# The 36 lead rows of V at the end of the V loop instead of evenly among the direct rows

## The chip, the core and the metric

The kernel runs on one core of a Trainium2 chip. The metric is the device time of one execution in microseconds (us). The changed kernel is timed in the same way as the kernel before.

## The reference

One encoder layer over two sequences (256 and 512 tokens, width 1024, treated as 6 tiles of 128 tokens): a norm, a projection to neighbourhood attention and retention heads, an output projection, a residual; then a second norm and a PEER layer (product-key expert retrieval), which is where this change lies:

```python
def block(args):
    xt, e, g = args              # tokens, 128 chosen experts of 16384 each, their gates
    ue = u[e]
    a = jax.nn.gelu(jnp.einsum('td,tkd->tk', xt, ue))
    ve = v[e]
    return jnp.einsum('tk,tkd->td', g * a, ve)
```

The experts stand in 128 rows of 128 experts each (`u` and `v` have 16384 x 1024 elements, float32).

## The kernel before, in words

The 768 tokens are two halves of 384 (3 tiles). PEER is computed in two ways.

**Scores of U.** In 256 steps TensorE multiplies one row of U (128 experts) with one half of the tokens: steps 0 to 127 for half 0, steps 128 to 255 for half 1. A step is 8 blocks of K by 3 products, since each operand is split into a high and a low part (`sp_hi`, `u_lo`; `ht_hi`, `ht_lo`): 24 matmuls of 384 columns (`scores`). ScalarE splits off the high part (`u_hi`), GpSimd the low part for steps up to 129 and VectorE from then on (`u_part`), and ScalarE applies the gelu into `act_g`, which has two buffers.

**Half 0 is sparse.** Its activations go to DRAM (`acts`), and each token's 128 chosen ones are gathered back. A *visit* n (384 of them: 3 tiles of tokens by 128 choices) is: GpSimd gathers the chosen V row of each of 128 tokens (`pick_v` into one of six `picked` slots, after visit n - 6 is done), and one activation per token (`pick_act` into `a_got`, 16 visits ahead); VectorE multiplies the row by its weight and adds it to `acc` or `acc_odd` (L1398).

**Half 1 is dense.** TensorE multiplies, for each of the 128 rows of V, the weights of all 384 tokens (activation times gate, `w_f`) with the row (`add_experts`): 3 tiles by 2 halves of the columns by 3 products, 18 matmuls of 512 columns. Its sums stay in PSUM through the whole loop.

**Lead rows and direct rows.** Steps 128 to 163 (rows 0 to 35 of half 1, `LEAD = 36`) are scored before the V loop, and their activations are stored to DRAM (`lead_acts`); these are the lead rows. In the V loop over q = 0 to 127 the row is `rows[q]`. For a lead row TensorE only runs `add_experts(q)`, and SyncE loads its activations back (`act_in`). For a direct row (36 to 127) TensorE first runs the score step of the next direct row and then `add_experts(q)`; the weights come straight from `act_g`.

**What sets the order.** All engines are programmed by hand and each runs its own instructions in order; semaphores join them. In a pass q of the V loop

- VectorE: a visit, `w_f` (L1416), a visit if the row has three, `w_lo` (L1421), for a direct row `u_lo` (L1433) of the row after next, a visit if the row has two or more, then `v_lo` (L1427) of q + 1.
- ScalarE: `w_hi` of q and then `v_hi` of q + 1, each of which waits until TensorE has ended the V matmuls that last read the same buffer (`y_done`, two rows back); for a direct row also the gelu of the next row and a `u_hi`.
- TensorE: for a direct row the scores of the next direct row, then `add_experts(q)`, which waits for `v_lo` and `w_lo` of q.
- SyncE (the SP queue): loads V for q + 2 after `v_lo` of q, the gates for q + 2 after `w_f` of q (`g_in`), the activations of the lead row two further on, and for a direct row a U row.
- GpSimd: only the gathers of the visits, with no tie to q but the `picked` slots.

`row_visits` says how many visits a row has: 3 for each direct row, and for a lead row 1, 2 or 3 (rows 0 and 3 three, rows 1, 2, 4, 5, 6 and those divisible by three from 9 on two, the others one). They sum to the 330 visits that are left when the loop begins (54 are made during the lead steps).

After the loop come the last sums, roots and outputs of half 0, then those of half 1.

Of the kernel before, what the change touches and what calls it, by code (L numbers as in the profile page):

```python
# [26 lines left out]
PEER_HEADS, TOPK, N_KEYS = 8, 16, 128  # L27
# [13 lines left out]
LEAD = 36  # L41
# [30 lines left out]
def encoder_program(nc, a):  # L72
# [3 lines left out]
    with ctx:  # L76
# [147 lines left out]

        rows, placed = [], {}
        for q in range(N_KEYS):
            early = q * LEAD % N_KEYS < LEAD
            n = sum(1 for row in rows if (row < LEAD) == early)
            rows.append(n if early else LEAD + n)
            placed[rows[q]] = q  # L230
# [1344 lines left out]
```

## Time and profile before

| | us |
|---|---|
| median of 3 runs | 2622.14 (2612.92 to 2632.96) |
| the profiled execution | 2621.9 |
| its span (first to last instruction) | 2620.1 |
| TensorE busy, matmuls (PE) | 2394.0 |
| VectorE busy (DVE) | 1719.4 |
| GpSimd busy (POOL) | 1356.0 |
| ScalarE busy (ACT) | 871.7 |

The profile is of one execution. Times in its rows are in us from the start of the span; a duration with "mean" is in ns. PE stands for TensorE's matmuls, PEld for its weight loads, DVE for VectorE, ACT for ScalarE, POOL for GpSimd, SP and SPq for SyncE and its DMA queue. Matmuls overlap one another in the trace (each row shows its latency), so what a group of matmuls costs is read from the starts. A row's bracket at the end is the engine's idle time before the instruction, and what ended it; "issue" is a gap in which the engine waited for nothing that the profile shows. L714 is line 714 of the kernel, the helper in which all score and V matmuls are issued. The V loop runs from about 1604 to 2603 us.

### The profile page before, as it was taken

How to read it: one execution, taken by the hardware profiler on the slowest of the kernel's cores; microseconds unless marked ns; L12 is line 12 of the kernel's file. 1: busy time of each engine (PE TensorE's matmuls, PEld its weight loads, DVE VectorE, ACT ScalarE, POOL GpSimd, SP SyncE). 2: the span in 40 equal slices, each digit the busy share in tenths (PEclk: the TensorE clock that was granted, in tenths of full speed). 3: DMA queues.
4: the chain of work that ended last, by engine and by line, in shares of the span. 5: the costliest groups of instructions: out<-in, count | busy, mean ns of one | idle time of the engine just before them, and what ended most of it. 6: DMA issues, size and time to landing. Idle time of an engine off the chain costs nothing.

```text
span 2620.1 us, 33731 instructions
## 1 busy us (share of the span) xinstructions
PE 2394.0 (91%) x12633; PEld 2158.4 (82%) x12633; DVE 1719.4 (66%) x3313; ACT 871.7 (33%) x1356; POOL 1356.0 (52%) x954
## 2 busy tenths in 40 slices
PE   5999998899999999999986877999999899999997
PEld 5977776799999999998976776887888788888886
DVE  4145437331798888555094956877887778777877
ACT  4234322232333333343332322333333333333333
POOL 1001130000266656644585545788778877888773
PEclk9999999989999999999998998999999999999998
DMA  4111102112455555537749598998999999988996
GB/s 143 65 47 46 56 33 81 57 65 89 151 171 171 176 185 180 166 130 219 231 151 356 176 303 286 322 356 312 323 321 325 316 320 325 322 317 302 330 320 232
DMA packets 233602, 555.10 MB, mean 212 GB/s; under 512 B 32064, under 2 KB 123200, under 8 KB 231776
## 3 DMA queue, kind: packets, MB, share of 16 engines
q1 hardware_dynamic: 164592, 345.04, 38.7%
q0 software_dynamic: 68848, 207.91, 22.7%
q8 instruction: 101, 1.65, 0.3%
q14 instruction: 61, 0.50, 0.1%
HBM read 483.90 MB, written 68.94 MB: 211 GB/s over the span
## 4 chain that ended last, share of the span: by engine, by line
PE 43%; POOL 26%; DVE 11%; DMA 8%; issue 8%; ACT 3%; SPq 1%; DVEq 0%; ACTq 0%; POOLq 0%
PE ps L714 25%; POOL a_got L466 12%; POOL picked L461 12%; PE ps L757 10%; DMA raw<-in_experts 4%; DVE hot_a L1341 4%; DMA picked<-in_experts,vidx 3%; POOL u_lo L472 2%; DVE hot_b L1337 2%; PE ps L793 2%; DVE acc_odd L1398 1%; PE ps L814 1%; ACT sp_hi L634 1%; DVE u_lo L1433 1%; PE ps L803 1%
## 5 line engine op out<-in xcount | busy, mean ns | idle before, releaser
L714 PE MATMUL ps<-ht_hi,sp_hi 128*128 128x384 f32 x2048 | 710.3, 347 | 48.6 <-DVE u_lo L1433 25.1
L714 PE MATMUL ps<-ht_hi,u_lo 128*128 128x384 f32 x2048 | 693.1, 338 | 0.0
L714 PE MATMUL ps<-ht_lo,sp_hi 128*128 128x384 f32 x2048 | 692.2, 338 | 0.0
L461 POOL DMA_INDIRECT picked<-in_experts,vidx x384 | 475.8, 1239 | 207.8 <-issue 108.1
L472 POOL TENSOR_TENSOR u_lo<-raw,sp_hi 128x1024 fp32r<-128x1024 f32 x130 | 340.6, 2622 | 418.6 <-ACT sp_hi L634 418.6
L466 POOL DMA_INDIRECT a_got<-acts,aidx x384 | 483.7, 1260 | 117.1 <-issue 117.0
L714 PEld LDWEIGHTS ps<-ht_hi,sp_hi 128*128 128x128 f32 x2048 | 389.3, 190 | 75.1 <-POOL u_lo L472 40.3
L714 PEld LDWEIGHTS ps<-ht_lo,sp_hi 128*128 128x128 f32 x2048 | 389.6, 190 | 3.6
L714 PEld LDWEIGHTS ps<-ht_hi,u_lo 128*128 128x128 f32 x2048 | 388.7, 190 | 0.0
L714 PE MATMUL ps<-v_hi,w_hi 128*128 128x512 f32 x768 | 311.3, 405 | 73.7 <-DVE w_lo L1421 57.8
L643 ACT ACTIVATE act_g<-ps 128x384 f32<-128x384 f32 x256 | 125.6, 491 | 609.4 <-PE ps L714 604.4
L714 PE MATMUL ps<-v_lo,w_hi 128*128 128x512 f32 x768 | 309.1, 402 | 0.0
L714 PE MATMUL ps<-v_hi,w_lo 128*128 128x512 f32 x768 | 309.1, 402 | 0.0
L634 ACT ACTIVATE sp_hi<-raw 128x1024 fp32r<-128x1024 f32 x256 | 269.5, 1053 | 103.7 <-DMA raw<-in_experts 103.6
L1398 DVE SCALAR_TENSOR_TENSOR acc<-picked,wts,acc 128x1024 f32<-128x1024 f32 x192 | 246.3, 1283 | 84.6 <-DMA picked<-in_experts,vidx 83.9
L1398 DVE SCALAR_TENSOR_TENSOR acc_odd<-picked,wts,acc_odd 128x1024 f32<-128x1024 f32 x189 | 243.1, 1286 | 67.2 <-DMA picked<-in_experts,vidx 66.7
L714 PEld LDWEIGHTS ps<-v_hi,w_hi 128*128 128x128 f32 x768 | 149.7, 195 | 116.2 <-issue 87.3
L1433 DVE TENSOR_TENSOR u_lo<-raw,sp_hi 128x1024 fp32r<-128x1024 f32 x126 | 153.5, 1218 | 81.5 <-ACT sp_hi L634 81.5
L986 DVE TENSOR_TENSOR sp_lo<-raw,sp_hi 128x1024 fp32r<-128x1024 f32 x52 | 63.3, 1223 | 199.2 <-ACT sp_hi L500 190.9
L1427 DVE TENSOR_TENSOR v_lo<-v_raw,v_hi 128x1024 fp32r<-128x1024 f32 x128 | 156.3, 1221 | 38.1 <-ACT v_hi L651 38.0
L757 PE MATMUL ps<-ht_hi,sp_hi 128*128 128x384 f32 x512 | 175.9, 344 | 5.3 <-DVE sp_lo L986 2.9
L688 ACT ACTIVATE w_hi<-w_f 128x384 fp32r<-128x384 f32 x128 | 67.1, 524 | 328.7 <-DVE w_f L1416 325.6
(183 smaller groups left out, 3431.4 us busy)
## 6 DMA issues: line engine op xcount, KB each, us to landing
raw<-in_experts SPq DMA_DIRECT2D x256, 512.0 KB, 3.9
v_raw<-in_experts SPq DMA_DIRECT2D x128, 512.0 KB, 5.5
raw<-in_front SPq DMA_DIRECT2D x52, 512.0 KB, 3.2
acts<-act_g SPq DMA_DIRECT2D x128, 192.0 KB, 3.5
gates<-stage SPq DMA_DIRECT2D x24, 1024.0 KB, 9.5
g_in<-gates SPq DMA_DIRECT2D x128, 192.0 KB, 5.4
lead_acts<-act_g SPq DMA_DIRECT2D x36, 192.0 KB, 5.4
act_in<-lead_acts SPq DMA_DIRECT2D x36, 192.0 KB, 5.6
```

The costliest lines, as they stand in the source:

```text
L461: pool.indirect_dma_start(picked[n % SLOTS][:, :], None, v_rows, bass.IndirectOffsetOnAxis(ap=vidx[:, n // P, n % P:n % P + 1], axis=0)).t ...
L466: pool.indirect_dma_start(a_got[:, n // P, n % P:n % P + 1], None, acts, bass.IndirectOffsetOnAxis(ap=aidx[:, n // P, n % P:n % P + 1], ax ...
L472: pool.tensor_tensor(u_lo[:, step % 2], raw[:, step % 2], sp_hi[:, step % 2].bitcast(F32), ALU.subtract).then_inc(S["u_lo"], 1)
L634: act.activation(sp_hi[:, step % 2], raw[:, step % 2], ACT.Copy).then_inc(S["u_hi"], 1)
L643: act.activation(act_g[:, step % 2], ps[:, step % 2, 0:HALF], ACT.Gelu_apprx_tanh).then_inc(S["gelu_done"], 1)
L688: act.activation(w_hi[:, q % 2], w_f[:, q % 2], ACT.Copy).then_inc(S["w_hi_ready"], 1)
L714: last = pe.matmul(out, l, r, start=start and k == 0, stop=stop and k == 2, skip_group_check=True)
L757: last = pe.matmul(ps[:, n % 2, 0:HALF], w, x, start=e == 0, stop=e == 23, skip_group_check=True)
L1341: last = dve.tensor_scalar(hot_a[:, g % HOT, q, :], s["iota"][:, :], idx_t[:, 0, t % 2, tok:tok + 1], idx_t[:, 2, t % 2, tok:tok + 1], ALU ...
L1398: last = dve.scalar_tensor_tensor(o[:, :], row, w, o[:, :], ALU.mult, ALU.add)
L1427: dve.tensor_tensor(v_lo[:, q % 2], v_raw[:, q % 2], v_hi[:, q % 2].bitcast(F32), ALU.subtract).then_inc(S["v_lo"], 1)
L1433: dve.tensor_tensor(u_lo[:, step % 2], raw[:, step % 2], sp_hi[:, step % 2].bitcast(F32), ALU.subtract).then_inc(S["u_lo_dve"], 1)
```

## The change

One line of the table that places the rows:

```diff
         rows, placed = [], {}
         for q in range(N_KEYS):
-            early = q * LEAD % N_KEYS < LEAD
+            early = q >= N_KEYS - LEAD
             n = sum(1 for row in rows if (row < LEAD) == early)
             rows.append(n if early else LEAD + n)
             placed[rows[q]] = q
```

Before, the order is 0, 36, 37, 38, 1, 39, 40, 41, 2, 42, 43, 3, and so on, to 35, 126, 127: a lead row after every two or three direct ones. Now it is 36 to 127, then 0 to 35. The number of visits of each row stays, and so do all instructions; GpSimd's order is the same, and those of TensorE, VectorE, ScalarE and SyncE are changed in the V loop.

VectorE at the beginning of the V loop, before (`acc_146` is the accumulator of the first tile of tokens, `picked_139` to `picked_144` are the six slots): the first pass is lead row 0 with three visits, the second is direct row 36.

```order
 L1427 TENSOR_TENSOR v_lo<-v_raw,v_hi 128x1024
 L1374 TENSOR_TENSOR wts<-a_got,sgate 128x8
 L1398 SCALAR_TENSOR_TENSOR acc_146<-picked_139,wts,acc_146 128x1024
 L1416 TENSOR_TENSOR w_f<-act_in,g_in 128x384
 L1398 SCALAR_TENSOR_TENSOR acc_odd<-picked_140,wts,acc_odd 128x1024
 L1421 TENSOR_TENSOR w_lo<-w_f,w_hi 128x384
 L1398 SCALAR_TENSOR_TENSOR acc_146<-picked_141,wts,acc_146 128x1024
 L1427 TENSOR_TENSOR v_lo<-v_raw,v_hi 128x1024
 L1398 SCALAR_TENSOR_TENSOR acc_odd<-picked_142,wts,acc_odd 128x1024
 L1416 TENSOR_TENSOR w_f<-act_g,g_in 128x384
```

The same place now:

```order
 L1427 TENSOR_TENSOR v_lo<-v_raw,v_hi 128x1024
 L1374 TENSOR_TENSOR wts<-a_got,sgate 128x8
 L1398 SCALAR_TENSOR_TENSOR acc_146<-picked_139,wts,acc_146 128x1024
 L1416 TENSOR_TENSOR w_f<-act_g,g_in 128x384
 L1398 SCALAR_TENSOR_TENSOR acc_odd<-picked_140,wts,acc_odd 128x1024
 L1421 TENSOR_TENSOR w_lo<-w_f,w_hi 128x384
 L1433 TENSOR_TENSOR u_lo<-raw,sp_hi 128x1024
 L1398 SCALAR_TENSOR_TENSOR acc_146<-picked_141,wts,acc_146 128x1024
 L1427 TENSOR_TENSOR v_lo<-v_raw,v_hi 128x1024
 L1398 SCALAR_TENSOR_TENSOR acc_odd<-picked_142,wts,acc_odd 128x1024
```

The first pass is a direct one: its weights come from `act_g`, and a `u_lo` stands between `w_lo` and the third visit.

VectorE at the end of the V loop, before (`acc_148` is the accumulator of the third tile; L1402 joins the two accumulators after the last visit): direct row 127 with three visits.

```order
 L1427 TENSOR_TENSOR v_lo<-v_raw,v_hi 128x1024
 L1398 SCALAR_TENSOR_TENSOR acc_odd<-picked_142,wts,acc_odd 128x1024
 L1416 TENSOR_TENSOR w_f<-act_g,g_in 128x384
 L1398 SCALAR_TENSOR_TENSOR acc_148<-picked_143,wts,acc_148 128x1024
 L1421 TENSOR_TENSOR w_lo<-w_f,w_hi 128x384
 L1398 SCALAR_TENSOR_TENSOR acc_odd<-picked_144,wts,acc_odd 128x1024
 L1402 TENSOR_TENSOR acc_148<-acc_148,acc_odd 128x1024
```

The same place now, lead rows 33, 34 and 35:

```order
 L1421 TENSOR_TENSOR w_lo<-w_f,w_hi 128x384
 L1398 SCALAR_TENSOR_TENSOR acc_odd<-picked_142,wts,acc_odd 128x1024
 L1427 TENSOR_TENSOR v_lo<-v_raw,v_hi 128x1024
 L1398 SCALAR_TENSOR_TENSOR acc_148<-picked_143,wts,acc_148 128x1024
 L1416 TENSOR_TENSOR w_f<-act_in,g_in 128x384
 L1421 TENSOR_TENSOR w_lo<-w_f,w_hi 128x384
 L1427 TENSOR_TENSOR v_lo<-v_raw,v_hi 128x1024
 L1398 SCALAR_TENSOR_TENSOR acc_odd<-picked_144,wts,acc_odd 128x1024
 L1402 TENSOR_TENSOR acc_148<-acc_148,acc_odd 128x1024
 L1416 TENSOR_TENSOR w_f<-act_in,g_in 128x384
 L1421 TENSOR_TENSOR w_lo<-w_f,w_hi 128x384
```

A lead row has a visit between `v_lo` and `w_f`, and a second one, where it has it, between `w_lo` and the next `v_lo`. The last visit and the joining of the accumulators now stand ahead of the last row's weights.

## Rows read from the trace of the kernel before

**Rows 1.** The page: busy time of each engine and its share of the span.

```profile
PE 2394.0 (91%) x12633; PEld 2158.4 (82%) x12633; DVE 1719.4 (66%) x3313; ACT 871.7 (33%) x1356; POOL 1356.0 (52%) x954
```

**Rows 2.** The page: the chain that ended last, shares of the span by line.

```profile
PE ps L714 25%; POOL a_got L466 12%; POOL picked L461 12%; PE ps L757 10%; DMA raw<-in_experts 4%; DVE hot_a L1341 4%; DMA picked<-in_experts,vidx 3%; POOL u_lo L472 2%; DVE hot_b L1337 2%; PE ps L793 2%; DVE acc_odd L1398 1%; PE ps L814 1%; ACT sp_hi L634 1%; DVE u_lo L1433 1%; PE ps L803 1%
```

**Rows 3.** Waits of GpSimd, 1700 to 2560 us: total, times, longest.

```profile
POOL a_got L466 <- issue: 85.5, 280, 0.3
POOL picked L461 <- issue: 82.4, 270, 0.3
```

**Rows 4.** Waits of all engines, 1605 to 2600 us.

```profile
PE ps L714 <- DVE w_lo L1421: 57.8, 35, 4.3
```

**Rows 5.** Timeline of VectorE at three places: start, duration, instruction.

```profile
1604.23 1.28 DVE L1398 SCALAR_TENSOR_TENSOR acc<-picked,wts,acc 128x1024 f32<-128x1024 f32 x1
...
2492.54 1.28 DVE L1398 SCALAR_TENSOR_TENSOR acc_odd<-picked,wts,acc_odd 128x1024 f32<-128x1024 f32 x1 [0.91 <-DMA picked<-in_experts,vidx]
...
2598.05 0.55 DVE L1421 TENSOR_TENSOR w_lo<-w_f,w_hi 128x384 fp32r<-128x384 f32 x1
```

**Rows 6.** VectorE, groups from 2492.5 to 2600 us: busy, mean ns, idle.

```profile
L1398 DVE SCALAR_TENSOR_TENSOR acc_odd<-picked,wts,acc_odd 128x1024 f32<-128x1024 f32 x19 | 24.4, 1285 | 8.0 <-DMA picked<-in_experts,vidx 7.8
L1398 DVE SCALAR_TENSOR_TENSOR acc<-picked,wts,acc 128x1024 f32<-128x1024 f32 x18 | 23.2, 1287 | 4.9 <-DMA picked<-in_experts,vidx 4.9
```

**Rows 7.** Timeline of TensorE's matmuls, starts of three groups.

```profile
2002.67 0.47 PE L714 MATMUL ps<-v_hi,w_hi 128*128 128x512 f32 x1 [1.02 <-DVE w_lo L1421]
...
2006.87 0.33 PE L714 MATMUL ps<-ht_hi,sp_hi 128*128 128x384 f32 x1
...
2011.05 0.39 PE L714 MATMUL ps<-v_hi,w_hi 128*128 128x512 f32 x1
```

**Rows 8.** Timeline of VectorE from 2000.8 to 2016 us.

```profile
2000.82 0.55 DVE L1416 TENSOR_TENSOR w_f<-act_in,g_in 128x384 f32<-128x384 f32 x1
2001.96 0.56 DVE L1421 TENSOR_TENSOR w_lo<-w_f,w_hi 128x384 fp32r<-128x384 f32 x1 [0.59 <-ACT w_hi L688]
2002.91 1.23 DVE L1427 TENSOR_TENSOR v_lo<-v_raw,v_hi 128x1024 fp32r<-128x1024 f32 x1 [0.39 <-ACT v_hi L651]
2004.05 1.28 DVE L1398 SCALAR_TENSOR_TENSOR acc<-picked,wts,acc 128x1024 f32<-128x1024 f32 x1
2005.25 0.60 DVE L1416 TENSOR_TENSOR w_f<-act_g,g_in 128x384 f32<-128x384 f32 x1
...
2007.44 1.22 DVE L1433 TENSOR_TENSOR u_lo<-raw,sp_hi 128x1024 fp32r<-128x1024 f32 x1
...
2011.53 1.29 DVE L1398 SCALAR_TENSOR_TENSOR acc_odd<-picked,wts,acc_odd 128x1024 f32<-128x1024 f32 x1 [0.42 <-DMA picked<-in_experts,vidx]
...
2015.81 1.29 DVE L1398 SCALAR_TENSOR_TENSOR acc<-picked,wts,acc 128x1024 f32<-128x1024 f32 x1 [2.53 <-DMA picked<-in_experts,vidx]
```

**Rows 9.** DMA, 1700 to 2560 us: queues (packets, MB, share), V loads.

```profile
q0 software_dynamic: 49249, 146.85, 48.3%
q1 hardware_dynamic: 47711, 129.13, 42.8%
...
v_raw<-in_experts SPq DMA_DIRECT2D x110, 512.0 KB, 5.5
```

**Rows 10.** Timeline of GpSimd from 2011 to 2015 us.

```profile
2011.09 0.94 POOL L461 DMA_INDIRECT picked<-in_experts,vidx  x1 [0.30 <-issue]
...
2013.94 0.94 POOL L461 DMA_INDIRECT picked<-in_experts,vidx  x1 [0.31 <-issue]
```

**Rows 11.** Timeline of ScalarE from 2001 to 2008 us.

```profile
2001.84 1.04 ACT L651 ACTIVATE v_hi<-v_raw 128x1024 fp32r<-128x1024 f32 x1
...
2007.13 1.06 ACT L651 ACTIVATE v_hi<-v_raw 128x1024 fp32r<-128x1024 f32 x1 [0.72 <-PE ps L714]
```

**Rows 12.** Busy time by stretch; the last three: granted clock, DMA share, GB/s.

```profile
1700.00:2560.00 860.00, 806.39 (x3870) 710.23 (x3869) 673.83 (x723) 281.07 (x377) 689.04 (x561) 0.98 0.91 322
```

**Rows 13.** Timeline of VectorE after the loop.

```profile
2607.59 3.48 DVE L1495 TENSOR_TENSOR x2d<-ps,x2d 128x1024 f32<-128x1024 f32 x3
```

## The prediction

> **What bounds the kernel now.** I read the busy line of the page first [rows 1]: TensorE is busy in 91% of the span and looks like the bound. The chain that ended last contradicts this for the last part of the kernel: a quarter of it is GpSimd's two gathers, `picked` and `a_got` [rows 2]. So the question is which engine sets the pace of the V loop, the stretch from 1604 us on, in which the order of the 128 V rows matters.
>
> GpSimd's waits between 1700 and 2560 us [rows 3] are only the gap of 0.3 us that stands before every gather: 168 us over 550 gathers. Nothing else is long enough to be named. GpSimd never stops, while TensorE waits 57.8 us for `w_lo` in the loop [rows 4]. One visit (a gathered V row for each of 128 tokens, and a gathered activation) costs GpSimd two gathers, and 384 visits are to be made.
>
> The pace: the first visit of the loop (number 54 of 0 to 383) starts at 1604.23 us [rows 5]. Number 347 starts at 2492.54 us, since 19 + 18 = 37 multiply-adds start from there on [rows 5, 6]. That is 293 visits in 888.3 us, 3.03 us each.
>
> TensorE's own price: the 18 V matmuls of a row take 4.2 us (2002.67 to 2006.87), the 24 score matmuls 4.2 us (2006.87 to 2011.05) [rows 7]. A direct row needs both, 8.4 us, a lead row 4.2 us. All rows need 92 x 8.4 + 36 x 4.2 = 924 us; from the first visit of the loop to the last `w_lo` (2598.05 us [rows 5]) it is 994. GpSimd asks 3 x 3.03 = 9.1 us for the three visits of a direct row, more than TensorE's 8.4. In the kernel before, one lead row comes for 2.56 direct ones: 3.56 rows hold 9.2 visits, 27.8 us of GpSimd, against 25.7 us of TensorE. TensorE runs ahead, waits about 1.6 us at each lead row (57.8 us in 35 waits), and GpSimd sets the time.
>
> **The change, part by part.** It moves rows, and adds or removes nothing. Loads, splits, matmuls and visits stay; GpSimd's order of instructions is the same. Each row keeps its visits: 3 for a direct row; for leads 3, 2, 2, 3, 2, 2, 2 (rows 0 to 6, 17 visits), then 1, with 2 for a row divisible by 3 (rows 7 to 35: 29 rows, 37 visits, 1.28 each).
>
> *Direct rows, 92 in a run.* GpSimd asks 9.1 us, TensorE 8.4, VectorE 3 x 1.28 + 2 x 1.22 + 2 x 0.55 = 7.4 [rows 8]. DMA stands below them: the software queue takes 48.3% of 860 us for 280 visits, 1.48 us each, the hardware queue 42.8% for 129 MB, 2.85 us per MB [rows 9]; a direct row with three visits and 1.25 MB of U, V and gates asks 8.0 us. So GpSimd stays the bound, and TensorE waits 0.7 us in each row. The leads, which gave GpSimd nothing to do beyond its pace but TensorE less work, no longer stand among them: TensorE loses 0.7 us 92 times, and keeps 36 short rows for the end.
>
> *Does GpSimd's pace itself move?* A gather takes 0.94 us while VectorE rests (2013.94 us [rows 10]; VectorE is idle for 2.53 us until 2015.81 [rows 8]), so a visit is at least 2 x (0.94 + 0.30) = 2.48 us; 0.55 of the 3.03 us come from gathers stretched beside VectorE's work. Per visit, that work is one multiply-add of 1.28 us and 1.24 us of splits and weights ((128 x 2.32 + 90 x 1.22) / 330). In the first 293 visits after the change the latter is (92 x 3.54 + 7 x 2.32) / 293 = 1.17 us. If splits and weights alone stretch gathers, 0.07 x 0.55 / 1.24 x 293 = 9 us are saved; if multiply-adds stretch them as much, half of it. The gather at 2011.09 us took 0.94 us beside the multiply-add of 2011.53 [rows 8, 10], which speaks for the first. Bounds 0 and 9, taken 8: visit 347 starts at 2492.5 - 8 = 2484.5 us.
>
> [...]
>
> *Lead rows 0 to 6* hold 2.4 visits each and stay at GpSimd's pace. Visit 347 is now the first of lead row 7 (54 + 92 x 3 + 17 = 347), so rows 0 to 6 lie within the count.
>
> *Lead rows 7 to 35, the new stage.* A row asks GpSimd for 1.28 x 3.03 = 3.9 us, DMA for 1.28 x 1.48 + 0.92 MB x 2.85 = 4.5, TensorE for 4.2. But no score matmuls stand between the V groups now, so what ScalarE and VectorE do between them is no longer covered. The pieces [rows 8, 11]: `w_f` to `w_lo` 1.14 us (2000.82, 2001.96), `v_hi` to `v_lo` 1.07 (2001.84, 2002.91), `v_lo` to the visit 1.14 (2004.05), visit to the next `w_f` 1.20 (2005.25). `v_hi` and `w_hi` are double, and those of row q+2 wait until TensorE has ended row q. This closes a loop over two rows: TensorE starts (2002.67), ScalarE's waiting `v_hi` starts 4.46 us later (2007.13), then 1.07 + 1.14 + 1.20 + 1.14, then 0.71 from `w_lo` to TensorE (2001.96 to 2002.67). Sum 9.72 us, 4.86 per row. Eight rows have a second visit between `w_lo` and the next `v_lo`, where VectorE is free for 0.9 us of the 1.2 (counted from TensorE's start of the row, `w_lo` has ended at -0.71 + 0.5 = -0.2, and `v_lo` can start at 4.46 - 4.86 + 1.07 = 0.67), so each adds 0.3 us: mean (21 x 4.86 + 8 x 5.16) / 29 = 4.94 us. V loads land in a median of 5.5 us [rows 9] and the loop leaves them 9.7 - 1.1 - 1.2 = 7.4; but some are slower, and the granted clock is 0.98 and not 1 [rows 12]. I allow 0.16 us: 5.1 us per row. Bounds: 4.43, the serial part on ScalarE and VectorE alone (`w_f` 2000.82 to 2005.25), and 5.6, if half of the V loads land 3 us late.
>
> *The queue.* On SP each lead row issues loads of V, gates and `act_in`, no U; the first two `act_in` loads come before the loop as now and lie ready for 92 rows. None is put behind a wait it did not have.
>
> *The tail.* Before: from the last `w_lo` (2598.05 [rows 5]) to the end 22.0 us, in which the last visit, the sum of the two accumulators and three outputs stand ahead of the additions at 2607.59 [rows 13], 9.5 us behind `w_lo`. Now the last visit stands ahead of the last weights, and the additions can start some 5.7 us behind `w_lo` (2 us of sums and roots, 3.7 of outputs): 22.0 - 3.8 = 18.2 us.
>
> **Sum.** 2484.5 + 2.3 (visit 347 to `w_lo` of row 7: 1.20 + 1.14) + 28 x 5.1 + 18.2 = 2647.8 us of span, and 1.8 us around it (the profiled execution took 2621.9 us with a span of 2620.1): **2650 us**. That execution stands at the median of the three runs (2622.1), so nothing is corrected. It is 28 us, 1.1%, slower.
>
> **The rivals.**
> 1. *No loss that can be measured.* If the loop over two rows does not bind, leads run at 4.43 us: 2484.5 + 2.3 + 124 + 18.2 + 1.8 = 2631 us. Or DMA and not GpSimd is the bound: its share is 0.91 [rows 12], the bytes do not change, and the end stays near 2620. Against the first stands the `v_hi` that waits for TensorE [rows 11]; against the second, that a gather with VectorE idle takes its shortest time under full DMA load.
> 2. *The lead stage stretches.* With a gap of 0.7 us in each row TensorE could be granted 1.2 instead of 2.4 GHz. The V matmuls of a row then take 4.2 us more, 2.1 us per row in the loop; over half of the stage 14 x 2.1 = 29 us, 2679 us. With late V loads, at 5.6 us per row, it is 2664. Against it: the granted clock is 0.98 with waits of 1.6 us at each lead row now.
> 3. *Faster: direct rows free GpSimd.* If a gather fell to 1.1 us there (2.8 us per visit), TensorE's 8.4 us would be the pace, visit 347 would start at 1604.2 + 293 x 2.8 = 2425 and the end be 2590. That needs 68 us saved where I find 8; it decides at 2.91 us per visit (visit 347 some 28 us earlier than I put it), below which the change is no loss. Nothing speaks for it: VectorE is busy for 7.4 of 9.1 us in a direct row, as densely as now (674 of 860 us).
>
> **How the numbers follow.** Forecast (2639 to 2662) 0.57; no loss (2620 to 2639) 0.21; stretch (2662 to 2688) 0.17; faster 0.05. About 1% (26 us) is what a measurement of this kernel can tell from no change. The line of 1% slower, 2648, lies within the forecast; 0.34 of its 0.57 go above it. Slower 0.34 + 0.17 = 0.51, same 0.23 + 0.21 = 0.44, faster 0.05. The range 2626 to 2684 leaves out the fast case, the DMA case and the far end of the stretch.
>
> **What would show it.** Right: GpSimd without waits until about 2480 us; TensorE waiting for `w_lo` 0.7 us in nearly each direct row; the 92nd row's visits done near 2433 us (17 visits before 2484.5); then GpSimd waiting for visits, leads 4.9 to 5.2 us apart, and `v_hi` waiting for TensorE. Wrong: leads 4.4 or over 5.6 us apart, `v_hi` waiting for its load, a clock well below 0.9 in the last 140 us, or direct rows 8.4 us apart.

## The result

The changed kernel is slower. Its median is 2673.1 us (2670.5 to 2691.1, 4 runs) against 2619.9 us (2612.9 to 2633.0, 4 runs) for the kernel before; the ratio is 1.022, with a 95% interval of 1.016 to 1.027. Timed again on another occasion (x4 below) it is 2669.9 against 2625.8 us, ratio 1.018 (1.014 to 1.023). I had forecast 2650 us, 1.1% slower, in a range of 2626 to 2684. So the time is in the range, but the loss of 53 us (44 in x4) is well above the 28 us forecast, and 2673 us stands where I had put the stretch of the lead stage (2662 to 2688, chance 0.17). A fifth execution of the changed kernel, of 2682.2 us, counts in the ratio and not in the median. The ratios, here and below, leave out executions more than 1.5% above the fastest of the same kernel, which are two of five in x1 and one of four in x8.

The profile taken with the result is of the execution of 2691.1 us, the slowest of the four. The one of x4 is of 2662.0 us. Both are used, and kept apart.

The page of the changed kernel, busy time of each engine and the chain by line, as [rows 1, 2]:

```profile
PE 2411.7 (90%) x12633; PEld 2160.4 (80%) x12633; DVE 1719.2 (64%) x3313; ACT 869.9 (32%) x1356; POOL 1380.3 (51%) x954
...
PE ps L714 22%; POOL a_got L466 12%; POOL picked L461 12%; PE ps L757 10%; DMA raw<-in_experts 5%; DVE hot_a L1341 4%; POOL u_lo L472 3%; DMA picked<-in_experts,vidx 2%; DVE hot_b L1337 2%; PE ps L793 2%; ACT sp_hi L634 1%; PE ps L814 1%; DVE acc L1398 1%; DVE acc_odd L1398 1%; DVE u_lo L1433 1%
```

The gathers' share of the chain is the same 12 + 12%. The matmuls' went from 25 to 22% of a longer span: nothing was added to TensorE's work, and what came is waiting.

GpSimd's waits from 1700 to 2560 us, as [rows 3], first profile of the changed kernel:

```profile
POOL a_got L466 <- issue: 83.0, 272, 0.3
POOL picked L461 <- issue: 80.3, 263, 0.3
POOL picked L461 <- DVE acc_odd L1398: 3.1, 8, 0.6
POOL picked L461 <- DVE acc L1398: 0.9, 2, 0.6
```

GpSimd has no waits but 4 us in the whole stretch, as forecast for the direct run. Then the same view of all engines in the lead stage, from x4 (2500 to 2640 us):

```profile
PE ps L714 <- DVE w_lo L1421: 18.4, 23, 1.5
POOL picked L461 <- DVE acc L1398: 16.8, 8, 4.2
...
POOL picked L461 <- DVE acc_odd L1398: 15.6, 13, 3.5
...
ACT v_hi L651 <- PE ps L714: 5.4, 8, 0.7
```

Here GpSimd waits 32 us for visits, and TensorE 18 us for `w_lo` in 23 rows: neither bounds the lead stage. (The first profile has 21 us for `w_lo` in 21 rows there, 2525 to 2668 us.) Three places of x4's VectorE timeline, as [rows 5]: the first visit of the loop, `w_lo` of lead row 7 (the 100th row), and `w_lo` of the last row.

```profile
1603.63 1.28 DVE L1398 SCALAR_TENSOR_TENSOR acc<-picked,wts,acc 128x1024 f32<-128x1024 f32 x1
...
2498.38 0.56 DVE L1421 TENSOR_TENSOR w_lo<-w_f,w_hi 128x384 fp32r<-128x384 f32 x1 [0.59 <-ACT w_hi L688]
...
2638.86 0.56 DVE L1421 TENSOR_TENSOR w_lo<-w_f,w_hi 128x384 fp32r<-128x384 f32 x1 [0.59 <-ACT w_hi L688]
```

Where the time went, in four profiles. The visits are numbered as in the prediction; visit 330 is the first after the direct run of the changed kernel. Each start is read from VectorE's timeline.

| | before | before again (x12) | after again (x4) | after |
|---|---|---|---|---|
| visit 54 starts | 1604.2 | 1603.3 | 1603.6 | 1606.0 |
| visit 330 starts | 2441.7 | 2434.4 | 2448.0 | 2472.0 |
| us per visit between | 3.03 | 3.01 | 3.06 | 3.14 |
| end of the span | 2620.1 | 2616.4 | 2660.2 | 2689.2 |
| from visit 330 to the end | 178.4 | 182.0 | 212.2 | 217.2 |
| lead rows 7 to 35, us per row | - | - | 5.02 | 5.14 |

Between x12 and x4, 30 us of the 44 come behind visit 330, where the changed kernel has its 36 lead rows with 54 visits, and the kernel before had the end of one direct row and 21 rows, 15 of them direct, with as many visits. The other 14 us are GpSimd's pace in the direct run. In the profile that came with the result the pace costs 30 us, and the lead stage 39.

### The profile page after: what moved, and what is told of

Its sections match the earlier page's. It is cut to its first block, busy times and chain, and to the rows that moved or that the text cites. A ratio compares the mean times of both kernels' runs of the same rounds, so it can differ in the third digit from the quotient of the medians.

```text
span 2689.2 us, 33731 instructions
## 1 busy us (share of the span) xinstructions
PE 2411.7 (90%) x12633; PEld 2160.4 (80%) x12633; DVE 1719.2 (64%) x3313; ACT 869.9 (32%) x1356; POOL 1380.3 (51%) x954
## 4 chain that ended last, share of the span: by engine, by line
PE 39%; POOL 27%; DVE 12%; DMA 9%; issue 8%; ACT 4%; SPq 0%; DVEq 0%; ACTq 0%; POOLq 0%
PE ps L714 22%; POOL a_got L466 12%; POOL picked L461 12%; PE ps L757 10%; DMA raw<-in_experts 5%; DVE hot_a L1341 4%; POOL u_lo L472 3%; DMA picked<-in_experts,vidx 2%; DVE hot_b L1337 2%; PE ps L793 2%; ACT sp_hi L634 1%; PE ps L814 1%; DVE acc L1398 1%; DVE acc_odd L1398 1%; DVE u_lo L1433 1%
## 5 line engine op out<-in xcount | busy, mean ns | idle before, releaser
L461 POOL DMA_INDIRECT picked<-in_experts,vidx x384 | 493.4, 1285 | 244.6 <-issue 108.9
L466 POOL DMA_INDIRECT a_got<-acts,aidx x384 | 489.2, 1274 | 117.0 <-issue 116.9
L714 PE MATMUL ps<-v_hi,w_hi 128*128 128x512 f32 x768 | 320.4, 417 | 119.8 <-DVE w_lo L1421 107.0
L714 PEld LDWEIGHTS ps<-v_hi,w_lo 128*128 128x128 f32 x768 | 152.3, 198 | 34.3
```

The source lines that it names most:

```text
L461: pool.indirect_dma_start(picked[n % SLOTS][:, :], None, v_rows, bass.IndirectOffsetOnAxis(ap=vidx[:, n // P, n % P:n % P + 1], axis=0)).t ...
L466: pool.indirect_dma_start(a_got[:, n // P, n % P:n % P + 1], None, acts, bass.IndirectOffsetOnAxis(ap=aidx[:, n // P, n % P:n % P + 1], ax ...
L714: last = pe.matmul(out, l, r, start=start and k == 0, stop=stop and k == 2, skip_group_check=True)
```

## The experiments

Times are medians; each ratio is to the kernel before, timed on the same chip. The executions of one kernel lie 4 to 17 us apart in most experiments, 22 in x4 and 36 in x10; those of the kernel before 12 to 35 us, by chip. In two kernels they part more widely: x1 took 2586 to 2596 or 2628 to 2635 us, x8 2574, 2603 or 2622 us. Profiles of both kinds exist for x1 alone (x1 and x11).

### x1 and x11: the same rows, the visits dealt out otherwise

```diff
-        row_visits = [3 if row >= LEAD else 1 for row in rows]
+        row_visits = [2 if row < LEAD or row % 5 == 0 else 3 for row in rows]
```

> The changed kernel (lead rows last) with the 330 visits of the V loop dealt out otherwise: every lead row has two, direct rows three, but those whose number is divisible by 5 two (18 of 92). Direct rows then hold 2.8 visits, lead rows 2. Theory (the time is lost because GpSimd, the bound in the direct run, has too little to do in the last 29 lead rows): GpSimd asks 2.8 x 3.1 = 8.7 us in a direct row and 6.1 us in a lead row, is never idle, and the time is that of the kernel before, 2610 to 2630 us. Rival 1 (lead rows in a run are slow by themselves, whatever visits they hold): 2655 us or more. Rival 2 (the loss is only the slower gathers of a run of direct rows, 3.14 us per visit against 3.03): 2640 to 2650 us.

Measured: 2587.7, 2586.1 and 2595.6 us, and 2628.3 and 2634.9 us; ratio 0.986 (0.984 to 0.988). The lead rows still stand last, and the whole loss is gone. More than that, the kernel is quicker than before. Neither rival holds. The slower two of the five are near the time of the kernel before, as the theory has it; the median of all five is 2595.6 us. The theory explains the return, not the gain, so the kernel was run once more for a profile of the quicker kind:

> x1 once more, since its profile is of an execution of 2635 us, while its others took 2586 to 2596 and 2628. Theory (two paces of GpSimd: gathers stretched while the direct run is GpSimd's, short once TensorE's regular beat leads): in a fast execution a visit costs 2.95 us or less in the direct run (8.3 us per row for 2.8 visits), a_got gathers take 1.1 us or less in the mean against 1.24 in the slow profile, and the lead stage takes the same in both. Rival (the lead stage is what differs): direct run as in the slow profile, lead rows under 5 us.

Measured: 2600.9 and 2586.1 us, on another chip than x1. GpSimd's groups from 1700 to 2360 us, first in x1 (the execution of 2634.9 us), then in x11 (2600.9 us): count, busy, mean ns, idle before.

```profile
L461 POOL DMA_INDIRECT picked<-in_experts,vidx x211 | 268.6, 1273 | 64.4 <-issue 61.9 <-DVE acc_odd L1398 2.4
L466 POOL DMA_INDIRECT a_got<-acts,aidx x212 | 263.2, 1241 | 64.7 <-issue 64.7
```

```profile
L461 POOL DMA_INDIRECT picked<-in_experts,vidx x224 | 259.3, 1158 | 101.1 <-issue 53.0 <-DVE acc_odd L1398 32.4 <-DVE acc L1398 15.7
L466 POOL DMA_INDIRECT a_got<-acts,aidx x224 | 230.6, 1030 | 68.5 <-issue 68.5
```

The activation gathers take 1241 ns in the mean in one and 1030 in the other, of the same program. Rows 36 to 91 of the loop stand 8.78 us apart in x1 (`w_lo` 1916.8 to 2399.5, 55 rows) and 8.31 in x11 (1918.0 to 2374.9), which is TensorE's price of a direct row. In x11 GpSimd waits 48 us for visits, in x1 2.4. The lead stage differs little (5.82 and 5.67 us per row). So the direct run has two paces: either GpSimd leads, and its gathers are stretched; or TensorE leads, and they are short. What makes a gather long or short is shown under x5 and x6.

### x2: the lead rows first

```diff
-            early = q >= N_KEYS - LEAD
+            early = q < LEAD
```

> The 36 lead rows at the beginning of the V loop instead of at the end, 3 visits in direct rows and 1 to 3 in lead rows as before. Theory (what costs is the clustering: GpSimd waits while lead rows with few visits pass, and bounds the direct rows): GpSimd idle in lead rows 7 to 35, then 276 visits at 3.1 us; as slow as with the leads last, 2650 to 2672 us, up to 15 us less because GpSimd enters the direct run six visits ahead. Rival (what costs is that the leads stand at the end of the program, where their loads, the last visits and the outputs meet): near the kernel before, 2615 to 2630 us.

Measured: 2660.4 us, ratio 1.014 (1.011 to 1.016). As the theory says; the end of the program has little to do with it. The waits of GpSimd while lead rows 7 to 35 pass (1660 to 1802 us):

```profile
POOL picked L461 <- DVE acc L1398: 32.4, 8, 12.3
POOL picked L461 <- DVE acc_odd L1398: 11.2, 14, 3.3
```

43.6 us of waiting for VectorE, lost at the beginning (12.3 of them in one wait), for which the direct rows behind pay: they go at GpSimd's pace to the end (9.19 us per row, `w_lo` 1802.0 to 2638.2 over 91 rows).

### x3: the loop over two rows made shorter

```diff
+                late = rows[q] < LEAD and row_visits[q] == 1
-                visits(1)
+                if not late:
+                    visits(1)
                 weights(q)
...
-                visits(row_visits[q] > 1)
+                visits(row_visits[q] > 1 or late)
```

> The changed kernel, in which a lead row with one visit makes it behind w_lo instead of between v_lo and w_f, so that the loop over two rows (v_hi, v_lo, visit, w_f, w_hi, w_lo, TensorE's group) is 1.2 us shorter for 20 of the last 29 rows. Theory (this loop sets the pace of the lead stage, 4.99 us per row in the changed kernel): 4.4 to 4.6 us per row, 10 to 15 us less than the changed kernel, which is 2673, so 2658 to 2663 us. Rival 1 (DMA sets the pace of the lead stage): 4.8 to 5.0 us per row, no change, 2670 us or more. Rival 2 (the picked rows arrive too late for an early visit): the gain is larger than 15 us, since the wait moves off the path as well.

Measured: 2660.9 us, ratio 1.013 (1.010 to 1.016); x4, on the same chip, 1.018. Lead rows 7 to 35 stand 4.69 us apart ((2635.3 - 2504.0) / 28) instead of 5.02, 9.2 us less in all, and the median is 8.9 us lower. The intervals overlap, so the time alone would not settle it; the rows' distance does. 4.69 us is more than the 4.4 to 4.6 us expected: `v_hi` waits for its V load in five rows here (5.5 us), in one in x4 (0.9 us). That is 0.16 us per row, which would account for it; it is not shown that nothing else does. (The 4.99 us for the changed kernel in the expectation was misread: it is 5.14 in the first profile.)

### x4 and x12: both kernels again

x4 is the changed kernel without an edit, x12 the kernel before.

> The changed kernel once more, on the same chip as the others. The profile that came with the result is of an execution of 2691 us, 18 us above the median of 2673. Theory: a visit costs 3.05 to 3.10 us in the direct run of a usual execution (3.14 in that profile), lead rows 7 to 35 stand 4.9 to 5.0 us apart in every execution, and the time is 2668 to 2676 us. Rival: the direct run is as slow as in that profile, and the lead stage is what varies.

> The kernel before once more, for its pace in another execution. Theory: 3.00 to 3.06 us per visit from visit 54 to 330, a_got gathers 1.24 us in the mean, GpSimd without waits, 2612 to 2633 us, the spread of its time following from the pace (330 visits times 0.03 us are 10 us).

Measured: x4 2669.9 us (2657.9 to 2680.3), x12 2618.3 us, one execution. The direct run is what varies most between the two profiles of the changed kernel: 3.06 and 3.14 us per visit, which is 22 us over 276 visits. The lead stage varies less, 5.02 and 5.14 us per row, 3.5 us over 28 rows, a little above the 4.9 to 5.0 expected: in the first profile `v_hi` waits for its V load in six rows (5.0 us), in x4 in one (0.9 us). GpSimd's activation gathers from 1700 to 2360 us, in x12, x4 and the first profile of the changed kernel:

```profile
L466 POOL DMA_INDIRECT a_got<-acts,aidx x218 | 265.8, 1219 | 66.6 <-issue 66.6
```

```profile
L466 POOL DMA_INDIRECT a_got<-acts,aidx x214 | 260.9, 1219 | 65.3 <-issue 65.3
```

```profile
L466 POOL DMA_INDIRECT a_got<-acts,aidx x207 | 268.5, 1297 | 63.2 <-issue 63.2
```

They take 1219, 1219 and 1297 ns; the V gathers (not shown) 1198, 1263 and 1274 ns. The pace follows the gathers' lengths.

### x5 and x6: what stretches a gather

x5 computes the low part of U in the V loop for 64 of 1024 columns; x6 shortens the multiply-adds of the visits in the same way.

```diff
+                n = D_MODEL if step < FIRST_DIRECT + 2 else 64
-                dve.tensor_tensor(u_lo[:, step % 2], raw[:, step % 2], ...
+                dve.tensor_tensor(u_lo[:, step % 2, 0:n], raw[:, step % 2, 0:n], ...
```

> The changed kernel with the low part of U in the V loop computed for 64 of its 1024 columns (the rest of u_lo is left as it was, so the scores of the direct rows are not the reference's): VectorE has 1.1 us less of two-input subtraction in each direct row, everything else is as before. In the second profile of the changed kernel a visit costs 3.06 us in the direct run, of which 2.48 are two gathers of 0.94 and their gaps. Theory (splits and weights stretch the gathers, 0.44 us per us; multiply-adds do not): 0.16 us less, 2.90 us per visit, 45 us less over 276 visits. Rival 1 (all two-input work stretches alike, 0.22 us per us): 2.98 us per visit, 22 us less. Rival 2 (the pace is not GpSimd's gathers but the landing of their data): 3.06 as before.

```diff
-                    last = dve.scalar_tensor_tensor(o[:, :], row, w, o[:, :], ALU.mult, ALU.add)
+                    n_cols = 64 if n >= VISITS - left else D_MODEL
+                    last = dve.scalar_tensor_tensor(o[:, 0:n_cols], row[:, 0:n_cols], w, o[:, 0:n_cols],
+                                                    ALU.mult, ALU.add)
```

> The changed kernel with the multiply-adds of the visits in the V loop done for 64 of 1024 columns (so the outputs of half 0 are not the reference's): VectorE has 1.1 us less in each visit; gathers are whole. Theory (multiply-adds hardly stretch the gathers): a visit stays at 3.0 to 3.06 us in the direct run, and the only gain is in the lead stage, whose loop over two rows holds one visit: 4.3 instead of 5.0 us per row, 20 us less in all. Rival (the port rule: a multiply-add with two SBUF inputs blocks the descriptor writing like a split): 0.24 us less per visit, 2.82, so that TensorE's 8.4 us per row bounds, 65 us less in the direct run besides.

Measured: x5 2626.7 us, 43 us below x4 (another chip, on which the kernel before took the same 2625.8 us), and 2.90 us per visit in the direct run (1608.5 to 2408.8 us, 276 visits), which is the theory's number. x6 (two executions) 2556.6 us, 113 us below x4: 2.75 us per visit (1606.1 to 2365.2), TensorE's pace, and 4.54 us per lead row. GpSimd's activation gathers in x6, same stretch as above:

```profile
L466 POOL DMA_INDIRECT a_got<-acts,aidx x238 | 236.0, 992 | 72.9 <-issue 72.9
```

992 ns, near the 940 of a gather beside an idle VectorE. The expectation for x6 fell: multiply-adds do stretch gathers, as its rival said. A multiply-add became 1.00 us shorter (1.28 to 0.28 us), and a visit at least 0.31 us (TensorE's pace hides the rest); in x5 a split became 1.00 us shorter (1.22 to 0.22 us), which is 0.33 us per visit, and a visit 0.16 us. So both count.

How they count is in the traces. VectorE and then GpSimd in x4:

```profile
1991.80 1.28 DVE L1398 SCALAR_TENSOR_TENSOR acc<-picked,wts,acc 128x1024 f32<-128x1024 f32 x1 [1.68 <-DMA picked<-in_experts,vidx]
...
1996.81 1.28 DVE L1398 SCALAR_TENSOR_TENSOR acc<-picked,wts,acc 128x1024 f32<-128x1024 f32 x1 [0.88 <-DMA picked<-in_experts,vidx]
...
1998.47 1.22 DVE L1433 TENSOR_TENSOR u_lo<-raw,sp_hi 128x1024 fp32r<-128x1024 f32 x1
```

```profile
1991.17 0.94 POOL L461 DMA_INDIRECT picked<-in_experts,vidx  x1 [0.30 <-issue]
1992.41 1.48 POOL L466 DMA_INDIRECT a_got<-acts,aidx  x1 [0.30 <-issue]
...
1997.05 1.86 POOL L461 DMA_INDIRECT picked<-in_experts,vidx  x1 [0.30 <-issue]
1999.21 1.30 POOL L466 DMA_INDIRECT a_got<-acts,aidx  x1 [0.30 <-issue]
```

The gather at 1991.17 starts while VectorE is idle and takes 0.94 us, though a multiply-add starts 0.63 us behind it. The one at 1992.41 meets that multiply-add with 0.67 us left (it ends at 1993.08) and takes 1.48. The one at 1997.05 meets a multiply-add with 1.04 us left and takes 1.86; the one at 1999.21 a split with 0.48 us left, and takes 1.30. Each time it is what is left of VectorE's instruction plus 0.81 or 0.82 us. So a gather is stretched only by the instruction that is under way when it starts; one that starts later does not matter.

All fourteen profiles show this between 1700 and 2360 us, where they hold 6046 gathers. 2513 of them meet a VectorE instruction that began at least 0.1 us before them and has at least 0.13 us left: in 2498 the length is what is left plus 0.82 us, within 0.03, with multiply-adds and splits alike. 1535 meet none with as much left, and none that starts within 0.1 us of them: all take 0.93 to 0.97 us, but one of 1.21. The other 1998 start within 0.1 us of the start of a VectorE instruction, and some of these are short and some long. The stretch of the pace is thus a matter of when the gathers start, and the two rates above are means over such starts.

### x7 and x8: GpSimd relieved, in both orders

Activations are gathered further ahead: two per visit while the 54 visits before the V loop are made, 0.83 per visit in it.

```diff
+            got = CHUNK
             for n in range(VISITS):
-                for k in ((CHUNK + 2 * n, CHUNK + 2 * n + 1) if n < CHUNK else (n + 2 * CHUNK,)):
-                    if k < VISITS:
-                        pick_act(k)
+                upto = min(VISITS, CHUNK + 2 * (n + 1) if n < 54 else max(118 + (n - 54) * 83 // 100, n + 12))
+                for k in range(got, upto):
+                    pick_act(k)
+                got = max(got, upto)
```

(and 12 semaphores `a_in` instead of 4).

> The kernel before (lead rows spread), but GpSimd gathers the activations further ahead: two per visit while the 54 visits before the V loop are made, where it waits some 100 us for VectorE, and then 0.83 per visit, so that it enters the loop 64 visits ahead in activations instead of 16. In the loop a visit costs it one V gather and 0.83 activation gathers for the most part, about 2.75 us instead of 3.03. Theory (GpSimd bounds the V loop of the kernel before): 2.8 x 2.75 = 7.7 us per average direct row, so TensorE's 924 us become the bound of the loop: 2560 to 2590 us. Rival 1 (GpSimd is not the bound, DMA is): no change, 2615 to 2625. Rival 2 (the lead steps become longer, since the earlier gathers load the DMA queues there): what the loop gains is lost before it, 2600 or more.

> The same with the lead rows last. Theory: the direct run goes at TensorE's 8.4 to 8.5 us per row (92 rows, 778 us), then lead rows 0 to 6 at 6.5 and 7 to 35 at 5.0 us (bound by the loop over two rows, 0.8 us per row above TensorE's price): 1604 + 778 + 45 + 145 + 21 = 2593 span, 2585 to 2600 us, 10 to 25 us behind the spread order, where the changed kernel is 45 us behind it. So placing the leads last costs less once GpSimd has slack. Rival (the cost of the placement is independent of GpSimd's pace): again 45 us behind the spread order.

Measured: spread, 2585.4 us (2575.4 to 2588.8), ratio 0.984 (0.977 to 0.990); leads last, 2588.9 us (2573.6, 2574.8, 2603.1 and 2621.7), ratio 0.986 (0.975 to 0.996). The difference between the orders, 44 us without this, cannot be told from zero with it: GpSimd's slack is what decides what the placement costs. In both, visit 54 starts 2 to 6 us later than without the earlier gathers (1609.7 and 1607.6 us), so little is lost before the loop. The difference between the orders is less than the 10 to 25 us that I expected. In the two profiles the direct run with the leads last wastes none of TensorE's time, and the spread order does. The stretch from 1700 to 2360 us in x7, x8 and x4: busy time of PE, PEld, DVE, ACT, POOL, then granted clock, DMA share, GB/s.

```profile
1700.00:2360.00 660.00, 643.30 (x3148) 573.17 (x3147) 549.13 (x594) 228.88 (x308) 530.85 (x423) 0.99 0.96 345
```

```profile
1700.00:2360.00 660.00, 660.00 (x3340) 601.23 (x3339) 560.87 (x588) 230.53 (x316) 497.55 (x438) 1.00 0.96 343
```

```profile
1700.00:2360.00 660.00, 613.73 (x3001) 547.80 (x3001) 503.62 (x530) 210.67 (x286) 529.73 (x428) 0.98 0.90 311
```

In x8 TensorE is busy in all 660 us, with 3340 matmuls against 3001 in x4. That gathers are short there is seen in VectorE's and GpSimd's timelines of x8 around 2010 us:

```profile
2002.54 1.28 DVE L1401 SCALAR_TENSOR_TENSOR acc<-picked,wts,acc 128x1024 f32<-128x1024 f32 x1
2004.87 0.56 DVE L1419 TENSOR_TENSOR w_f<-act_g,g_in 128x384 f32<-128x384 f32 x1 [1.05 <-ACT act_g L646]
...
2010.77 1.28 DVE L1401 SCALAR_TENSOR_TENSOR acc_odd<-picked,wts,acc_odd 128x1024 f32<-128x1024 f32 x1
2013.18 0.62 DVE L1419 TENSOR_TENSOR w_f<-act_g,g_in 128x384 f32<-128x384 f32 x1 [1.13 <-ACT act_g L646]
2013.72 1.27 DVE L1401 SCALAR_TENSOR_TENSOR acc<-picked,wts,acc 128x1024 f32<-128x1024 f32 x1
```

```profile
2003.66 0.98 POOL L467 DMA_INDIRECT a_got<-acts,aidx  x1 [0.30 <-issue]
...
2011.96 0.94 POOL L467 DMA_INDIRECT a_got<-acts,aidx  x1 [0.30 <-issue]
2013.21 0.94 POOL L462 DMA_INDIRECT picked<-in_experts,vidx  x1 [0.30 <-issue]
```

VectorE waits 1.13 us for `act_g`, TensorE's product, in nearly every row (84 us in 76 rows from 1700 to 2360 us), and an activation gather starts as that gap opens: at 2011.96 us, where the multiply-add has 0.09 us left, and one row earlier at 2003.66, where it has 0.16, 8.30 us apart like the two `w_f`. In x8 159 of 198 activation gathers are shorter than 1 us, in x4 90 of 213; in x11 it is 167 of 224, in x1 78 of 211. When GpSimd leads, VectorE waits for picked rows instead, at places that change. That the regular beat is what puts the starts of gathers there is argued from these rows, and fits x1 and x11; no run forced the one pace or the other with all else equal.

### x9 and x10: both placed on top

x9 has x8's gathers and x1's visits, x10 x8's gathers and x3's late visit.

> Lead rows last, visits dealt out as in x1 (2.8 per direct row, 2 per lead row) and activations gathered ahead as in x8. In x8's profile the direct run goes at TensorE's 8.30 us per row with three visits each, and executions fall into two groups (2574 and 2603 to 2622 us). Theory (GpSimd bounds only while its gathers are stretched; with 2.8 visits instead of 3 per direct row it has 0.5 us more slack per row): all executions in the fast group; lead rows with two visits are bound by VectorE at 5.2 us, so 2570 to 2580 us. Rival (the two groups have nothing to do with GpSimd's slack): a spread of 30 us or more again, median 2585 to 2600.

> x8 with the late visit of x3 in lead rows with one visit. Theory (the two changes add, since one acts on the direct run and the other on the lead stage): 9 us less than x8 in the same group of executions, 4.7 instead of 5.0 us per lead row: 2563 to 2568 us where x8 has 2574. Rival (the lead stage is bound by loads once GpSimd is ahead): 5.0 us per lead row as in x8, 2573.

Measured: x9 2594.9 us (2593.5 to 2598.8), ratio 0.988 (0.984 to 0.993): the four executions agree within 5 us, as the theory says, but 15 us above its figure, at a median that its rival gave. The direct run is at 8.31 us per row (`w_lo` 1907.5 to 2364.4, 55 rows), the lead rows with two visits at 5.83 instead of the 5.2 I had from VectorE's work. VectorE's and TensorE's waits there, 2410 to 2570 us:

```profile
PE ps L717 <- DVE w_lo L1424: 35.7, 23, 7.3
...
DVE wts L1377 <- DMA a_got<-acts,aidx: 13.1, 4, 6.3
```

Thirteen us are waiting for activations that were not gathered far enough ahead any more (four waits of VectorE), and the DMA share is 0.95 from 2430 to 2560 us. x10: 2582.2 us (2563.7 to 2599.9), ratio 0.983 (0.976 to 0.991), and 4.76 us per lead row ((2555.6 - 2422.2) / 28) against 5.02 in x8, 7 us less. The mechanism is as expected, but the median does not stand clear of x7's and x8's. x10, x7 and x8 are all quicker than both kernels of this case; which of them is best these runs can't tell.

## Why the prediction was right, and where it was off

**The bound.** Right. GpSimd sets the pace of the direct run, not TensorE, though TensorE is busy in over 90% of it: x7 and x8 take GpSimd's work and nothing else out of the loop, and 40 us (x7) and 81 us (x8 against x4, on another chip) go.

**Where the loss comes from.** Right for 30 of the 44 us between x12 and x4, and shown from two sides. The visits of the direct rows are too many for GpSimd, those of the last lead rows too few to keep it busy. x1 moves visits, not rows, and the loss is gone; x2 moves the rows to the other end, and most of it stays. The other 14 us (30 in the first profile) are GpSimd's pace in the direct run, for which I had forecast a small gain.

**The lead stage.** The loop over two rows gave 4.94 us per row, with 0.16 allowed for late loads and the clock; measured 5.02 and 5.14. ScalarE's and VectorE's timelines of x4 show the distances that the sum was made of:

```profile
2603.32 0.56 DVE L1421 TENSOR_TENSOR w_lo<-w_f,w_hi 128x384 fp32r<-128x384 f32 x1 [0.59 <-ACT w_hi L688]
2604.33 1.23 DVE L1427 TENSOR_TENSOR v_lo<-v_raw,v_hi 128x1024 fp32r<-128x1024 f32 x1 [0.45 <-ACT v_hi L651]
2605.48 1.28 DVE L1398 SCALAR_TENSOR_TENSOR acc_odd<-picked,wts,acc_odd 128x1024 f32<-128x1024 f32 x1
2606.68 0.55 DVE L1416 TENSOR_TENSOR w_f<-act_in,g_in 128x384 f32<-128x384 f32 x1
2607.82 0.56 DVE L1421 TENSOR_TENSOR w_lo<-w_f,w_hi 128x384 fp32r<-128x384 f32 x1 [0.59 <-ACT w_hi L688]
```

```profile
2608.49 1.06 ACT L651 ACTIVATE v_hi<-v_raw 128x1024 fp32r<-128x1024 f32 x1 [0.70 <-PE ps L714]
```

From `w_lo` 2603.32 to the next, 2607.82, it is 4.50 us: the serial part on ScalarE and VectorE (4.43), and behind it the `v_hi` at 2608.49 that had to wait 0.70 us for TensorE, so that the next row takes 5.24 (to 2613.06). These two rows together make 9.74, the 9.72 of the sum. Behind a row with two visits the distance is 5.15 (2613.06 to 2618.21), and `v_hi` waits for nothing there: VectorE's own instructions are the path. The mean is within 0.1 us of the forecast in x4. x3, which takes the visit out of the loop, and x6, which shortens it, both move the distance. I had the number of second visits slightly wrong: the rows 0 to 6 hold 16 visits, not 17, and nine rows from 7 on have a second visit, not eight; visit 346 and not 347 is then the first of row 7, worth 3 us.

**GpSimd's pace.** The step that failed. I took 8 us off before visit 347, since there is less splitting per visit in direct rows. Measured, visit 347 starts at 2500.5 us in x4 and 2525.9 in the first profile, not at 2484.5: 16 and 41 us later. A visit costs 3.06 and 3.14 us in the direct run, where it cost 3.03 and 3.01. Two things were wrong. I took it that splits and weights alone stretch gathers, at 0.44 us per us. x6 and the rows of x4 above show that multiply-adds count alike. The gather of 0.94 us beside a multiply-add, on which I rested this ([rows 8, 10]), started at 2011.09 us, 0.44 us ahead of the multiply-add of 2011.53, and so says nothing about it. And the pace does not follow from the amount of work: what counts is what VectorE has under way when a gather starts. For starts at random moments I estimate, from the 0.82 us and VectorE's durations of 1.28, 1.22 and 0.55 us, a stretch of 0.38 us per gather in either order; measured are 0.29 and 0.27 in the two profiles of the kernel before (from the means), 0.30 in x4 and 0.35 in the first profile. So the amount of work would have moved nothing. The same program runs at 8.78 or 8.31 us per row (x1, x11). Why the starts fall worse in an unbroken direct run than in one broken by lead rows is open.

**The tail.** 18.2 us taken, 21.3 measured in x4 (`w_lo` 2638.86 to 2660.2). ScalarE's timeline there:

```profile
2638.31 0.52 ACT L688 ACTIVATE w_hi<-w_f 128x384 fp32r<-128x384 f32 x1 [4.22 <-DVE w_f L1416]
2638.74 1.04 ACT L704 ACTIVATE junk<-acc 128x1024 f32<-128x1024 f32 x1
...
2639.96 1.06 ACT L704 ACTIVATE junk<-acc 128x1024 f32<-128x1024 f32 x1
...
2641.21 1.06 ACT L704 ACTIVATE junk<-acc 128x1024 f32<-128x1024 f32 x1
...
2642.38 1.28 ACT L516 ACT_TABLE_LOAD   x1
```

The three squares stand behind the last `w_hi` in ScalarE's order, and a table load of 1.28 us behind them. I had freed VectorE's side and let the outputs start 2 us behind `w_lo`; the squares alone take 3.6 us (2638.74 to 2642.38), and the outputs start 5.3 us behind `w_lo`. The 2 us came from no row; the 3.7 us of outputs are right (3.67 in x4).

**The sum** for x4, from `w_lo` of row 7 on: it came 11.6 us later than summed (2498.4 against 2486.8), the 28 rows took 2.3 less, the tail 3.1 more: 12.4 us in all, and 2647.8 + 12.4 = 2660.2. For the first profile it is 37.1 us later (2523.9), the 28 rows took 1.2 more, the tail 3.1: 41.4, and 2647.8 + 41.4 = 2689.2. The range held the result because it was wide enough for a term with the wrong sign; that part was luck. The interval that the result fell into was meant for a stretched lead stage, and that did not come.

**The signs.** The waits of TensorE in the direct run are fewer and longer than I said: 54.1 us in 36 waits up to 2440 us in x4, not 0.7 us in each row. `v_hi` waits for TensorE in eight rows from 2500 us on, not in every second one. Visit 330 starts at 2448.0 us in x4 and 2472.0 in the first profile, where I had about 2433. The granted clock is 1.00 in x4 from 2500 to 2639 us; in the lead stage of the first profile it is 0.94 from 2525 to 2555 us and 1.00 behind that, so nothing came of the rival with 1.2 GHz. Late loads came to little: 5.0 us of waits of `v_hi` in the first profile, 0.9 in x4.

## What to carry to other kernels

When two kinds of pass alternate and an engine with a queue of its own feeds both, price each kind for each engine, not only the average: clustering costs when the engine that bounds one kind has to wait while the other kind passes, and what it costs depends on that engine's slack (x8). Work that is tied to passes can be moved instead of the passes, and often at once repairs more than the order did (x1). The busiest engine need not be the bound: here TensorE was busy in over 90% of the direct run, and GpSimd, which hardly waited, set the pace. And where two engines disturb each other, look in the timeline at what is under way when the disturbed instruction starts, before you count the amount of work beside it.

## What was not expected of the hardware

- A GpSimd gather of 128 rows takes 0.94 us if VectorE is idle when it starts; if it starts during an instruction of VectorE, it takes what is left of that plus 0.82 us, whether that is a multiply-add or a subtraction (2498 of 2513 gathers within 0.03 us). What VectorE starts later does not lengthen it. So the mean depends on where the starts fall: 1030 and 1241 ns for the activation gathers of the same program in two executions (x11, x1), on two chips; executions on one chip part by 30 us or more of the whole time (x1).
- The Trainium skill (SBUF — State Buffer, "SBUF: two separate sides") says that VectorE and GpSimd share one port pair as an exclusive lock, that whoever starts first has it for the whole instruction, and that a VectorE instruction with two SBUF inputs takes it only against a GpSimd operation that reads SBUF. This case agrees for VectorE's instructions: a gather that starts during one is held until it ends (1997.05 in x4). The gathers take their indices from SBUF (`vidx`, `aidx`). It does not agree the other way round: the gather of 0.94 us at 1991.17 in x4 does not keep the multiply-add of 1991.80 from starting, nor does that one take longer than its 1.28 us.
- DMA went on at 343 to 345 GB/s with a share of 0.96 in x7 and x8, so the 0.91 of the kernel before was near its end but was not the bound.
